# The moving rows and the outputs of a streamed fp32r product, walked from the last column to the first

## What is computed

```python
h = rms_norm(x, norm_mix[l]);  proj = h @ w_in[l]                 # 2048 x 5120
a, o, yc = attention(proj), hgrn2(proj), short_conv(proj)         # small against the rest
x = x + jnp.concatenate([a, o, cb * yc], axis=-1) @ w_out[l]      # 2048 x 2048
h = rms_norm(x, norm_ffn[l])
gate, up = jnp.split(h @ w_gate_up[l], 2, axis=-1)                # 2048 x 11264
x = x + (jax.nn.silu(gate) * up) @ w_down[l]                      # 5632 x 2048
```

## Time and profile before

| | |
|---|---|
| median of three runs | 2547.03 us |
| the profiled execution | 2545.48 us |
| its span, first to last instruction | 2543.9 us |
| TensorE matmul busy | 2529.2 us, 99% |
| TensorE weight loads busy | 2501.4 us, 98% |
| VectorE busy | 1476.0 us, 58% |
| ScalarE busy | 1015.7 us, 40% |
| GpSimd busy | 331.1 us, 13% |
| DMA | 420.84 MB, 165 GB/s |
| mean granted TensorE clock | 0.999 of 2.4 GHz |

### The profile page before, as it was taken

The page is one execution under the profiler, slowest core; times in us unless marked ns, Lnnn a source line. Parts: engine busy times, 40 slices in busy tenths (PEclk is TensorE's granted clock), DMA queues, the critical chain, the costliest instruction groups (busy, mean ns, idle before and its releaser), DMA issues.

```text
span 2543.9 us, 51052 instructions
## 1 busy us (share of the span) xinstructions
PE 2529.2 (99%) x19426; PEld 2501.4 (98%) x19426; DVE 1476.0 (58%) x2011; ACT 1015.7 (40%) x1412; POOL 331.1 (13%) x279
## 2 busy tenths in 40 slices
PE   9999999999999999999999999999999999999998
PEld 9999999999999999999999999999999999999998
DVE  6678787555554445555545787775555444555544
ACT  5454554333333333333334545443333333333333
POOL 3011003111110011111100200131111000111111
PEclk9999999999999999999999999999999999999999
DMA  6545445444455454454455554454455554444553
GB/s 233 172 160 182 157 142 172 157 165 165 165 172 167 157 165 165 165 165 166 165 166 166 177 174 153 141 166 166 165 165 165 165 167 163 165 165 165 167 165 136
DMA packets 116516, 420.84 MB, mean 165 GB/s; under 512 B 13840, under 2 KB 15120, under 8 KB 116368
## 3 DMA queue, kind: packets, MB, share of 16 engines
q1 hardware_dynamic: 109296, 397.72, 47.4%
q0 software_dynamic: 4112, 14.78, 1.8%
q10 hardware_dynamic: 3024, 7.16, 0.9%
HBM read 411.06 MB, written 11.87 MB: 166 GB/s over the span
## 4 chain that ended last, share of the span: by engine, by line
PE 97%; DVE 2%; ACT 1%; DMA 0%; issue 0%; DVEq 0%; SPq 0%
PE gp L1604 31%; PE gp L1608 31%; PE gp L1606 31%; PE mb L1657 1%; PE mb L1768 0%; PE mb L1781 0%; PE mb L1789 0%; DMA raw<-wstream 0%; PE mb L1666 0%; ACT sc L567 0%; PE mb L1715 0%; DVE wlo L770 0%; PE mb L1732 0%; ACT sc L565 0%; PE mb L1843 0%
## 5 line engine op out<-in xcount | busy, mean ns | idle before, releaser
L770 DVE TENSOR_TENSOR wlo<-raw,whi 128x1024 fp32r<-128x1024 f32 x754 | 987.4, 1343 | 362.4 <-ACT whi L430 359.1
L430 ACT ACTIVATE whi<-raw 128x1024 fp32r<-128x1024 f32 x754 | 768.1, 1051 | 583.8 <-PE gp L1608 550.0
L1604 PE MATMUL gp<-xh,whi 128*128 128x288 f32 x4096 | 885.4, 297 | 1.3 <-issue 0.8
L1608 PE MATMUL gp<-xl,whi 128*128 128x288 f32 x4096 | 879.3, 296 | 0.0
L1606 PE MATMUL gp<-xh,wlo 128*128 128x288 f32 x4096 | 874.2, 295 | 0.0
L1604 PEld LDWEIGHTS gp<-xh,whi 128*128 128x128 f32 x4096 | 657.7, 188 | 9.2 <-issue 6.9
L1606 PEld LDWEIGHTS gp<-xh,wlo 128*128 128x128 f32 x4096 | 657.2, 188 | 0.0
L1608 PEld LDWEIGHTS gp<-xl,whi 128*128 128x128 f32 x4096 | 656.5, 188 | 0.0
L1608 PE MATMUL gp<-fl,whi 128*128 128x288 f32 x1408 | 303.2, 296 | 0.0
L1604 PE MATMUL gp<-fh,whi 128*128 128x288 f32 x1408 | 301.0, 294 | 0.0
L1606 PE MATMUL gp<-fh,wlo 128*128 128x288 f32 x1408 | 301.0, 295 | 0.0
(11 more groups left out here) (266 smaller groups left out, 1653.8 us busy)
## 6 DMA issues: line engine op xcount, KB each, us to landing
raw<-wstream SPq DMA_DIRECT2D x754, 512.0 KB, 4.2
s<-s_cache POOLq DMA_DIRECT2D x8, 512.0 KB, 10.7
hs_out<-s ACTq DMA_DIRECT2D x8, 512.0 KB, 3.3
caches_out<-caches POOLq DMA_DIRECT2D x8, 496.0 KB, 8.8
x<-x_in ACTq DMA_DIRECT2D x4, 576.0 KB, 8.6
kct<-kt_cache POOLq DMA_DIRECT2D x4, 512.0 KB, 6.2
vct<-v_cache POOLq DMA_DIRECT2D x4, 512.0 KB, 7.0
y_out<-x SPq DMA_DIRECT2D x3, 576.0 KB, 2.9
```

Of the source, the lines that this page charges most:

```text
L430: a.activation(whi[slot][:], raw[slot][:], ACT.Copy).then_inc(hi_ready, 1)
L770: v.tensor_tensor(wlo[slot][:], raw[slot][:], whi[slot][:].bitcast(F32), ALU.subtract).then_inc(lo_ready, 1)
L1604: t.matmul(outs[c], whi[slot][:, k, c * P:(c + 1) * P], mv_hi, start=first, stop=False)
L1608: mm = t.matmul(outs[c], whi[slot][:, k, c * P:(c + 1) * P], mv_lo, start=False, stop=end)
```

## The change

A helper is added that makes, from a row of 288 columns, the access pattern that starts at column 287 and steps by minus one. `block` applies it to both moving rows and to both outputs. So column 287 of the activations is read first and lands in column 287 of PSUM, written first; the data that stand in PSUM after a product are in the same places as before. The stationary side, the order and number of products, the waits and all other products stay.

```diff
+        def backwards(row):
+
+            return bass.AP(row.tensor, row.offset + TOK - 1, [row.ap[0], (-1, TOK)])
...
             def block(slot, k, sides, bank, mv, first, end):

-                mv_hi, mv_lo = mv
-                outs = [gp[2 * bank + c][:, 0:TOK] for c in range(2)]
+                mv_hi, mv_lo = (backwards(v_) for v_ in mv)
+                outs = [backwards(gp[2 * bank + c][:, 0:TOK]) for c in range(2)]
                 for c in sides:
                     t.matmul(outs[c], whi[slot][:, k, c * P:(c + 1) * P], mv_hi, start=first, stop=False)
```

## The result

The changed kernel takes 2550.62 us (median of 19 runs, 2550.44 to 2552.50) against 2546.62 us (19 runs, 2545.04 to 2547.17). The ratio is 1.002, with a 95% interval of 1.0013 to 1.0027. It is slower by a little, and a ratio of 1 lies outside the interval.

The account below looks back on a forecast made before the run. TensorE's dense stream was taken as the bound: 18048 x 132.6 ns = 2393 us, plus 151 us unedited. The profiled 2545.48 us, plus 18048 x 0 for the change and 1.55 us to the median, gave 2547.0 us; range 2538 to 2775 us.

Parts of the forecast that it names:

- The sign that I had named: Products per 200 us between 600 and 1200 us: a count leaving 1505 to 1512 would prove the forecast wrong.
- What bounds the kernel: Whole span: TensorE, busy 99%, sets the time through one dense line of products, 132.6 ns each.
- the count: The block's three lines: 6016 products each, 18048 in all, every one touched by the change.
- what is not touched: Outside the stream: mixers' small products, start and end, 151 us unedited; no instruction, wait or weight changes.
- I take zero: Every product of the stream: walking the 288 columns downwards adds nothing, 18048 x 0.
- rival B: Every product of the stream: backward start costs a fixed price, for example a late line; up to +227 us, chance 0.15.
- Is there cover?: Weight loads beside the stream: can start every 111 ns, 21 ns below the interval, so no lengthening is hidden.
- The lower end: Bound on the new walk's price: all time above pure column time vanishes from every product, -227 us.
- the 12.6 ns: Each stream product: the part of its 132.6 ns interval above 120.0 ns for 288 columns; cause unknown.

Follow-up runs that it names:

- pairs: Changed kernel with both sides stepping backwards in pairs of columns (286, 287, 284, 285 and so on): 2552.07 us, ratio 1.0021.
- fours: Changed kernel with both sides stepping backwards in runs of four columns (284 to 287, 280 to 283 and so on): 2550.50 us, ratio 1.0019.

## Why the prediction was wrong

I had forecast 2547.0 us and no change, with 0.65 on less than 0.2% either way; it is 1.002 (1.0013 to 1.0027) times the kernel before, just on that bound and clearly on the slow side. 2550.62 us lies inside the stated range, which is no merit: the range reached to 2775 us for a rival whose top price of 227 us is some 45 times what was measured. The sign that I had named didn't speak either. The counts after are 1505, 1506 and 1506, inside the 1505 to 1512 within which I wasn't to be wrong, though the whole 0.2% is in them: that window was too wide by the size of the effect.

**What bounds the kernel, the count, and what is not touched** held. TensorE's line is dense in both, 18048 products, and every tenth of a nanosecond in the interval reaches the end: 0.28 ns gave 5 us.

**The step that failed is "I take zero"**, the price of the new walk. I looked for it in each side by itself, an address unit that takes neighbours in falling order, and on that the evidence was right: PSUM takes them for nothing, and pairs, fours and single steps cost the same. The term that was missing is the meeting of the moving row's reads with the weight load's. It measured 0.28 ns per product at this placement. As a sum it had the form of rival B, a small price per product, but B's mechanism (a line fetched late at the start), which asks nothing of the weights, doesn't fit: in the pure stretches the price is gone with still weights, and it turns into a gain of 18 us where all rows stand 64 bytes off (2546.57 us upwards, with the 1.4 us wait at the start in it, and 2527.09 us downwards, without).

**Is there cover?** I reasoned that the weight side, able to start every 111 ns, doesn't set the interval, and left it out of all that followed. The conclusion doesn't hold: what the weight side reads moves the interval (6401 products, 6454 with still weights), though by that estimate it had 21 ns to spare.

**The lower end** said nothing excludes a gain, "as I don't know what the 12.6 ns are". That was the right doubt, and the place to dig. 8.4 ns of them go when the row stands still.

**The rule of the Trainium skill** ("Advanced Engine Details and Errata", Memory Cachelines) that access patterns which are not contiguous significantly slow products in PSUM is not borne out for steps of minus one, nor for pairs or fours walked down: writing down alone gave a ratio of 1.0 (0.9991 to 1.001). The page "TensorE: Matmul & The Clock Gate" (Part 2: What happens when you issue a matmul) says that loading the next weights doesn't steal read bandwidth from the running product. Here the runs differ from it by about 1%: weights at one address bring 6454 products where 6401 fitted.

**Not settled:** what in SBUF or TensorE makes the two readers meet, and why the intervals lie on a ladder of 6 to 7 ns. The runs show that distance, direction and order matter, and suggest that what precedes a stretch does. No model here gives the level in advance. ScalarE, VectorE and the DMA queues use SBUF at the same time, and no run kept them still; the still-weights kernels, in which their work goes on and the price is gone from 400 to 1250 us, speak against them as its cause there without ruling them out.

## What to carry to other kernels

In a dense stream of products, the placement of moving rows against weights in SBUF and the order in which a row is read are settings worth trying: here they moved the same computation from 2550.6 to 2527.1 us, and to 2521.3 us in one run, without one instruction more or less. Count products in a pure window to judge them; one trace shows a step of 0.2% that a few timed runs on two levels blur. And price a change of access against everything that reads at the same time, not against the operation alone.

## What was not expected of the hardware

- The stream's interval is one of few values, held for hundreds of slabs to within 1 ns: 3153, 3160, 3173, 3180, 3187 or 3193 ns per 24 products (and 3147 ns in 23 slabs of one kernel). Inside a slab the products are unevenly spaced, 127 to 138 ns in the kernel before.
- At the same addresses it can hold either of two (3173 and 3187 ns, upwards at 64 bytes), in different parts of one run.
- Products whose moving row stands still take 124.4 ns each, 8.4 ns less than with one that walks; still weights save 1.1 ns.
- PSUM written from the last column to the first costs nothing that the trace can show (6400 against 6401 products in 850 us).
